# Two-layer streaming encoder on one core: indexer and group A scores in head pairs, output projections in the turned banks

## The reference

```python
# group A: 8 query heads, 2 kv heads; keys picked by a 4-head indexer
dots  = einsum('bqhd,bld->bqhl', iq, ik_all)                 # 4 indexer heads, 64 wide
score = einsum('bqh,bqhl->bql', iw, relu(dots)) * IDX_SCALE  # one score per query and key
score = where(admissible, score, -inf)                       # chunk-causal
_, idx = top_k(score, 256)
s = einsum('bqngd,bqknd->bqngk', qg, k_sel) * 64 ** -0.5     # 2 kv heads x 4 query heads
o_a = einsum('bqngk,bqknd->bqngd', softmax(s), v_sel)
# group B: 4 heads, 1 kv head, a window of 3 chunks of 64, a sink per head
# group M: 4 heads over 256 memory tokens
y = concat([o_a, o_b, o_m]) * silu(gate)
x = x + einsum('btm,md->btd', y, w_out)                      # 1024 -> 1024
```

## Time and profile before

| what | value |
|---|---|
| median of 3 runs | 1681.35 us (1676.07 to 1683.68) |
| profiled execution | 1682.72 us, span 1680.9 us |
| PE busy | 1509.8 us, 90% of the span |
| PE weight loads (beside the products) | 832.3 us, 50% |
| DVE busy | 907.1 us, 54% |
| ACT busy | 659.9 us, 39% |
| POOL busy | 161.2 us, 10% |
| DMA | 114 MB, mean 68 GB/s |
| L697 PE, QUERIES/GATE/KEYS and OUT | 388.4 + 234.0 us |
| L827 PE, scores of A | 183.8 us |
| L794 PE, scores of the indexer | 93.7 us |

### The profile page before, as it was taken

The page is one execution under the profiler, slowest core; times in us unless marked ns, Lnnn a source line. Parts: engine busy times, 40 slices in busy tenths (PEclk is TensorE's granted clock), DMA queues, the critical chain, the costliest instruction groups (busy, mean ns, idle before and its releaser), DMA issues. The chain is left out here.

```text
span 1680.9 us, 19527 instructions
## 1 busy us (share of the span) xinstructions
PE 1509.8 (90%) x6364; PEld 832.3 (50%) x6364; DVE 907.1 (54%) x2361; ACT 659.9 (39%) x1628; POOL 161.2 (10%) x191
## 2 busy tenths in 40 slices
PE   2999999999859999999779999999995799999992
PEld 1544456666524455544434444666664345555451
DVE  0444527887526566656224444488773456666543
ACT  1223426776523333433112242477664233343332
POOL 0100013300000000000001000132000000000003
PEclk9999799999879999999779997999997899999986
DMA  7211310120322111111051004003005121111106
GB/s 270 56 41 33 133 47 1 57 83 40 139 55 53 51 51 51 51 51 25 22 193 40 22 29 153 25 1 113 39 39 170 36 72 51 51 51 51 25 11 235
DMA packets 122623, 114.04 MB, mean 68 GB/s; under 512 B 56432, under 2 KB 95056, under 8 KB 122448
## 3 DMA queue, kind: packets, MB, share of 16 engines
q1 hardware_dynamic: 122528, 112.84, 20.9%
HBM read 87.13 MB, written 30.10 MB: 70 GB/s over the span
## 5 line engine op out<-in xcount | busy, mean ns | idle before, releaser
L697 PE MATMUL score_ps<-w_slot,hT 128*128 128x512 f32 (+2 forms) x1024 | 388.4, 538 | 5.5 <-DMA w_slot<-in_w_in_dram 5.1
L697 PEld LDWEIGHTS score_ps<-w_slot,hT 128*128 128x128 f32 x1024 | 195.8, 194 | 186.3 <-issue 180.2
L1055 ACT ACTIVATE hT<-hT,neg_top 128x128 f32<-128x128 f32 (+8 forms) x144 | 118.0, 820 | 413.6 <-DVE neg_top L1314 413.1
L697 PE MATMUL score_ps<-w_slot,work 128*128 128x512 f32 x512 | 234.0, 611 | 23.4 <-issue 23.4
L1209 DVE TENSOR_SCALAR_CACHE_REDUCE work<-bias,trial 128x384 f32<-128x384 f32 (+3 forms) x256 | 226.0, 883 | 6.8
L922 ACT ACTIVATE work<-bias,neg_trial 128x768 bf16<-128x768 f32 (+2 forms) x192 | 198.4, 1043 | 67.4 <-DVE neg_trial L1205 67.4
L827 PE MATMUL score_ps<-akT,query_mem 64*128 64x512 f32 (+4 forms) x448 | 183.8, 533 | 7.4 <-ACT prob_bm L1069 6.7
L1305 DVE CUSTOM_DVE_ANT_0 hT<-score_ps,bias 128x128 f32<-128x128 f32 (+8 forms) x144 | 116.1, 806 | 116.3 <-PE score_ps L827 115.1
L697 PEld LDWEIGHTS score_ps<-w_slot,work 128*128 128x128 f32 x512 | 97.1, 195 | 147.2 <-issue 146.9
L768 PE MATMUL score_ps<-hT,w_slot 128*128 128x352 f32 x448 | 135.2, 460 | 1.4 <-ACT gate_raw L1044 1.4
L1110 POOL TENSOR_TENSOR work<-work,norm_sb 128x512 f32<-128x512 f32 (+1 forms) x36 | 42.6, 1183 | 915.9 <-DMA norm_sb<-norm_scratch 915.9
(11 more groups left out here) (181 smaller groups left out, 1741.0 us busy)
## 6 DMA issues: line engine op xcount, KB each, us to landing
gate_raw<-x_scratch SPq DMA_DIRECT2D x32, 512.0 KB, 3.7
w_slot<-in_w_in_dram SPq DMA_DIRECT2D x8, 2048.0 KB, 9.5
gate_scratch<-gate_raw SPq DMA_DIRECT2D x16, 528.0 KB, 2.7
w_slot<-in_w_out_dram SPq DMA_DIRECT2D x4, 2048.0 KB, 10.9
work<-gate_scratch SPq DMA_DIRECT2D x16, 512.0 KB, 4.5
norm_sb<-norm_scratch SPq DMA_DIRECT2D x64, 128.0 KB, 3.3
x_scratch<-gate_raw SPq DMA_DIRECT2D x16, 512.0 KB, 3.7
hT<-x_scratch SPq DMA_DIRECT2D x8, 512.0 KB, 8.0
```

The lines of the kernel that those rows point to most:

```text
L697: last = nc.tensor.matmul(out[:, 0:cols], lhs(k), w[:, k, 0:cols], start=(k == 0), stop=(k == KD - 1))
L1055: nc.scalar.activation(p, p, ACT.Exp, bias=neg_b[0:r, j:j + 1], scale=SM_SCALE, accum_out=sums[t % 2][0:r, sum_cols(i, j):sum_cols(i, j) + ...
```

## The change

- **Indexer.** An INDEX step becomes (tile, pair of heads, 512 keys). The two heads of a pair lie in the two 64-row halves of the array and their products stand one behind the other, into columns 0 to 511 and 512 to 1023 of one score buffer. ACT takes two relus per step, DVE adds two. Tiles with up to 512 keys have two steps, those with 640 to 1024 four, the sample six. The wait for the stores of k and v goes from INDEX to TOPK.
- **Group A scores.** Item (A,g) is now query heads 2g and 2g+1 of both kv heads. QK steps come in rounds of two: the products of the two heads alternate between the two halves and the two score buffers, and the steps before PE's need both buffers free. The PV products of A are 64x128 each, twice as many.
- **OUT** goes into the turned banks, c = 0 into one and c = 1 into the other. It has a turn number of its own, so it waits for the copy of the turn two before it, and the turn two behind it waits for ADD. The ADD step goes behind the next round of QK.
- **MIX** of B and M goes behind the PT pair that follows.
- **SP**: half 0 of the output weights is loaded after four of the eight gate stores; tile 1's rows and half 1 of the weights come behind the two round trips of tile 0.

The diff, cut:

```diff
@@ groups_of
+    if item[1] == "A":
+        ...
+            flat = [(g, b, w) for g in range(2) for b, w in whole]
+            cut = [flat[k:k + 2 * at_once] for k in range(0, len(flat), 2 * at_once)]
+        return [[(2 * u + g, b, w) for g, b, w in part for u in range(2)] for part in cut]
@@ attention_steps
-        nxt = score_steps(i + 2) if i + 2 < len(ITEMS) else []
+        nxt = score_rounds(i + 2) if i + 2 < len(ITEMS) else []
...
                 steps.append(("OUT", t - 1, c))
                 if t + 1 in SEARCHED:
                     steps.append(("MASK", SEARCHED.index(t + 1), c))
-                steps.append(("ADD", t - 1, c))
+                added.append(("ADD", t - 1, c))
             while given < len(nxt) and given * groups <= g * len(nxt):
-                steps.append(nxt[given])
+                steps += nxt[given] + added
+                added = []
...
+                        (last_mixes if s[0] == "MIX" and s[2] else steps).append(s)
@@ plan
+def index_steps(t):
+    return [("INDEX", t, hp, c) for hp in range(IDX_HEADS // 2) for c in range(-(-NKEYS[t] // 512))]
@@ numbered
-        if s[0] in ("MEM", "KEYS", "INDEX", "QUERIES", "GATE", "QK", "OUT", "EXTRA"):
+        if s[0] in ("MEM", "KEYS", "INDEX", "QUERIES", "GATE", "QK", "EXTRA"):
...
-        for q in range({"NORM": 2, "CACHE": 1, "MEM_T": 1, "KEYS_T": 2, "QUERIES_T": 2, "PT": 1
+        for q in range({"NORM": 2, "CACHE": 1, "MEM_T": 1, "KEYS_T": 2, "QUERIES_T": 2, "PT": 1, "OUT": 1
@@ sync
-                    for c in range(2):
-                        sp.dma_start(w_slot[c]...).then_inc(w_out_loaded, 16)
+                        if f == KD // 2 - 1:
+                            w_out_load(0)
...
                     tile_load(0)
-                    tile_load(1)
                     for t in range(TILES):
                         norm_turn(t, 1)
                         norm_turn(t, 0)
-                        if t:
+                        if t == 0:
+                            w_out_load(1)
+                            tile_load(1)
+                        else:
@@ tensor, INDEX
+                            for u in range(2):
+                                half = slice(HD * u, HD * (u + 1))
+                                last = nc.tensor.matmul(out[0:r, 512 * u:512 * u + w],
+                                                        iqT[half, hp, t * P:t * P + r],
+                                                        ikT[half, k0:k0 + w], start=True, stop=True)
@@ tensor, QK
+                                for c in range(0, m, 512):
+                                    w = min(512, m - c)
+                                    for u, out in enumerate(pair):
+                                        half = slice(HD * u, HD * (u + 1))
+                                        last = nc.tensor.matmul(out[0:r, c:c + w], aqT[half, head, t * P:t * P + r],
+                                                                akT[half, k0 + c:k0 + c + w], start=True, stop=True)
@@ tensor, OUT
-                            out = score_buffer(step)
-                            pe.wait_ge(w_out_loaded, 32)
+                            g = turn_use(step)
+                            pe.wait_ge(turn_free[g % 2], g // 2)
+                            out = turn_ps[g % 2].rearrange("p k n -> p (k n)")
+                            pe.wait_ge(w_out_loaded[step[2]], 16)
@@ scalar, INDEX
+                            for k in range(2):
+                                at = slice(512 * k, 512 * k + w)
+                                ins = nc.scalar.activation(index_relu[u % 2][0:r, at], ps[0:r, at], ACT.Relu,
+                                                           scale=iw_abs[0:r, t, 2 * hp + k:2 * hp + k + 1])
```

More of the change, by code:

```diff
@@ L89, in score_steps, with score_rounds @@
     return [("QK", i, j) for j in range(4 if ITEMS[i][1] == "A" else 1)]
+def score_rounds(i):
+    steps = score_steps(i)
+    return [steps[k:k + 2] for k in range(0, len(steps), 2)]
 def attention_steps():
-    steps, late, waiting, held = [], [], [], []
+    steps, late, waiting, held, last_mixes = [], [], [], [], []
     last_group = (len(ITEMS) - 1, len(groups_of(ITEMS[-1])) - 1)
@@ L123, in attention_steps @@
         for g in range(groups):
+            added, made = [], []
             if t and it[1:] + (g,) in OUT_AT[t == SMP]:
@@ L152, in attention_steps @@
             waiting += made
+    steps += last_mixes
     while late:
@@ L177, in plan @@
         steps += index[3:4] + [("ROPE", t)]
-    steps += [("INDEX", NT - 1, h) for h in range(IDX_HEADS)] + [("KEYS_T", SMP)]
+    steps += index_steps(NT - 1) + [("KEYS_T", SMP)]
+    last = index_steps(SMP)
     for h, filler in enumerate([("QUERIES", 0), ("MEM", 0), ("MEM", 1)]):
-        steps += [filler, ("INDEX", SMP, h)]
-    steps.append(("INDEX", SMP, IDX_HEADS - 1))
+        steps += [filler] + last[2 * h:2 * h + 2]
+    assert len(last) == 6
     steps += [("TOPK",), ("MEM_T", 0), ("MEM_T", 1)]
@@ new lines, in _ @@
+                            if what == "A":
+                                if j % 2:
+                                    continue
+                                pair = [score_buffer(step), score_buffer(("QK", i, j + 1))]
+                                k0, m, head = 0 if t < SMP else SEQ, min(NKEYS[t], 1024), 2 * g + j // 2
+                                for c in range(0, m, 512):
[4 more added lines that the diff above has]
+                                                                akT[half, k0 + c:k0 + c + w], start=True, stop=True)
+                                        if c + w == m:
+                                            last.then_inc(score_full, 1)
+                                continue
@@ new lines, in _ @@
+                            out = score_buffer(step)
+                            for hh in range(4):
+                                half = HD * (hh % 2)
+                                rows = slice(half, half + HD)
+                                if what == "B":
+                                    q = bqT[rows, hh // 2, t * P:t * P + r]
+                                    k0 = SEQ if t == SMP else P * max(t - 1, 0)
+                                    k = bkT[rows, k0:k0 + (P if t == 0 else 2 * P if t < SMP else P + DEC)]
+                                else:
+                                    q = mqT[rows, hh // 2, t * P:t * P + r]
+                                    k = mkT[rows, int(t == SMP), hh // 2, :]
+                                last = nc.tensor.matmul(out[0:r, 256 * SLOT[hh]:256 * SLOT[hh] + k.shape[1]], q, k,
+                                                        start=True, stop=True)
@@ L1285, in _ @@
+                            if hp == IDX_HEADS // 2 - 1 and 512 * c + w == n and t < SMP:
+                                link(nc.vector.memset(s[0:CHUNK, w - CHUNK:w], NEG))
                         elif kind == "TOPK":
+                            for b in range(2):
+                                dve.wait_ge(kv_stored[b], 16 * kv_dmas(b, TILES))
                             for t in range(TILES):
@@ L1381, in _ @@
                             r, cols = ROWS[t], slice(512 * c, 512 * (c + 1))
-                            ps, free = scores(("OUT", t, c))
+                            bank, free = turned(("OUT", t, c))
+                            ps = bank.rearrange("p k n -> p (k n)")
                             loads = len(range(t % 2, NORMS, 2)) + t // 2 + len(x_parts(t))
```

148 lines of the change are left out of this document (59 added, 89 removed).

## The result

The changed kernel takes **1760.22 us** (median of 4 runs, 1756.41 to 1765.07) against 1679.71 us before (4 runs): ratio 1.0492, 95% interval 1.0463 to 1.0522. The forecast was 1693 with a range to 1730. The direction was right and the size was not: +80 us came where +12 were expected.

The account below looks back on a forecast made before the run. PE's work was taken to bound attention. Per layer 13.4 - 9.1 - 9.0 + 10.5 = +5.8, two layers +11.6 on the profiled 1682.7, 1694, less 1.4 to the median: 1693 us; range 1648 to 1730 (8 in 10).

Parts of the forecast that it names:

- the indexer's term: Indexer: paired products save PE time, mostly at tiles 6 and 7; -9 us per layer, bounds +3 and -17.
- the walk through attention: Attention: hand walk of the new order with old durations, new PE waits against saved work; +13.4 us per layer.
- the clock: Attention: waits of 1.65 us or more bring half-clock drops, nine at 1.15 us each; +10.5 us per layer.
- The pair at the price of one head: A's scores and indexer: two halves run at once, so a pair costs PE 1.98 us at 1024 columns, like one head.
- The rival of a dearer pair: Rounds and indexer steps: a pair costs more than one head, +15 to 20 us, about 1710; chance 0.05.
- The waits of tile 6: Attention, tile 6: new PE waits of together 12.85 us against less work, so 54.8 us instead of 50.2.
- The same walk for the other tiles: Attention: tile 7 +4.6 us, tile 4 +3.5, tiles 1, 2, 3, 5 and the sample within 0.8 of before.
- The start of attention: Before the first OUT: fewer loads ahead shorten the first round trip, OUT at 482.3; -9.1 us per layer.
- the bound called 0: Start of attention: half the weights still ahead and the first trip taking its old 13.5 us; stated as 0, noted "5 less".
- The fourth: Attention: clock falls between OUTs and stays low, tile 6 under 0.85; 1712 to 1730 us, chance 0.16.

Follow-up runs that it names:

- e6: Changed kernel with copies of turned banks and ADD moved between the first and second head of a round on ACT and DVE: 1704.75 us.
- e5: Changed kernel with ADD ahead of the next round of scores, OUT still in the turned banks: 1723.08 us.
- e12: e6 with ACT's copies of turned banks also moved ahead of the exponentials of B, at all tiles: 1679.18 us.
- e2: Kernel before with only the indexer in head pairs of 512 keys: 1677.23 us, ratio 0.9978.
- e1: Kernel before with only the changed order of loads: 1664.91 us, ratio 0.9906.
- e3: Kernel before with OUT in the turned banks and ADD behind the next head's scores, heads still single: 1769.55 us.
- e8: Kernel before with the changed order of loads and the paired indexer, nothing else: 1666.03 us, ratio 0.9916.
- e4: Changed kernel with OUT back in the score buffers and ADD ahead of the next round; pairs, paired indexer and load order stay: 1698.93 us.
- e7: e4 with copies of turned banks and ADD between the first and second head of a round on ACT and DVE: 1672.29 us.
- e11: e8 (single heads) with ACT's copies of turned banks ahead of the exponentials of B and M where they follow directly: 1652.19 us.

## Why the prediction was wrong

The step that failed first is the indexer's term: PE time was taken as saved wherever PE had been busy. The other two terms that failed, the walk through attention and the clock, had the right mechanism and were too small. All errors lean to the same side. In us per layer:

| term | forecast | layer 0 | layer 1 |
|---|---|---|---|
| to the last gate store (indexer) | -9.0 | 0.0 | +2.0 |
| from there to the first OUT | -9.1 | -7.6 | -7.6 |
| attention without the clock's cost (the walk) | +13.4 | +24.7 | +24.5 |
| the clock's cost in attention | +10.5 | +17.4 | +22.4 |
| behind it | 0 | +1.2 | +1.1 |
| sum | +5.8 | +35.7 | +42.4 |

**The pair at the price of one head.** Right: 1.99 us for a pair of 1024 keys. The rival of a dearer pair is out.

**The waits of tile 6.** Right in sum and, but for one, in cause. The walk had 0.35, 2.2, 2.7, 3.05, 1.65, 0.2 and 2.7, in sum 12.85; PE is idle for 12.84, and the large waits are 0.40, 2.16, 2.99, 2.96, 1.47 and 2.71. The 1.65 was to be a round that waits for M's scores. The trace has 1.47 before a turn, for ACT's copy behind two exponentials; that the sizes agree is luck. In e6 that turn no longer waits, and the next round waits 1.50 us for M's exponentials. The other causes are shown by the runs that move them. In e5 the 2.96 for ADD becomes 1.35 and 0.47 for copies. In e6 the 2.16 becomes 0.96, and the 2.71, which was for ACT's copy, becomes 1.46 for MIX. In e12 the 2.99 is gone.

**The same walk for the other tiles.** Here the sum fell short. Without the clock's cost, attention of layer 0 went from 318.5 to 343.2 us: +24.7 instead of +13.4. Of the 11.3 us missing, 6 are in tiles 1 to 3, where I had forecast nothing (+0.6, -0.4, -0.25) and each became some 2 us longer (+2.2, +1.8, +2.0 without the clock's cost), and 2.1 in tile 7 (+6.7 against +4.6). Tile 2 stands idle for 6.5 us of its 37.5: 1.90 for ADD, 1.54 for M's exponentials, 1.22 and 1.03 before OUT for copies, 0.79 before M's scores. So the small tiles have the kinds of wait that the large ones have. That they have less PE work to hide them is my reading; no run takes it apart.

**The clock.** The mechanism was right and the term of +10.5 per layer too small. I took nine drops of 3.4 us. Attention of layer 0 has twelve stretches below full clock, where it had three before, so nine more is what came. Ten of them last 3.4 to 4.3 us and cost 1.5 to 1.7 us each; the others are that of the first OUT and one of 21 us at the sample, of which 15 us lie in attention and cost 6.6 (4.3 before). I had counted each drop at 1.15 because the next wait would give back a third. At the full 1.7 nine drops are 15 us, and that is most of what was missing in layer 0. In tile 6, with two drops, the waits add up to the 12.84 us that the walk had without any, so there nothing was given back. Layer 1 has two more stretches of some 7 us (3.0 and 2.6) near its end.

**The indexer.** The step that failed outright: -9 per layer was forecast, and to the end of the gates layer 0 came out 0.5 us shorter; alone (e2) the pairs gave 2.6 us in both layers. I let PE's saved time count wherever PE had been busy, though the turns and projections wait for copies on DVE that stand behind the indexer's sums. 15 us less busy time became 17 us more idle time.

**The start of attention.** Right in cause, near in size: the second half of the first trip was issued at 464.78 and that of the second at 475.88, forecast 465 and 475.3; the first OUT came at 483.77, forecast 482.3. From the last gate store to the first OUT the gain is 7.6 us in both layers against the 9.1 forecast, and 8.8 and 8.5 in e1, where nothing else is changed (15 us in all). In the prediction the bound called 0 is worked out as 5 less; that slip changed nothing.

**The rivals.** The fourth (clock low for long) describes the sample's 21 us and e3's 18 us, but tile 6 had a granted clock of 0.94, not under 0.85, so it isn't what made the 80 us. Those are, for a layer, 24.6 of waits less saved work, some 20 of clock, less 6 to 8 up to the first OUT. The upper end of 1730 failed because terms that lean to the same side were each taken at their middle: indexer 9 to 11, walk 11, clock 7 to 12, start 1.5 and the way behind attention 1 make 30 to 37 per layer.

**What the two parts of the attention change are worth.** With the new loads and the paired indexer everywhere: single heads, OUT in score buffers 1666 (e8); pairs, OUT in score buffers 1699 (e4); pairs, OUT in turned banks 1760 (after). Against before without those two: single heads, OUT in turned banks 1770 (e3). In attention of layer 0 e3 and the changed kernel differ by -34 us of work and +35 of idle time, at about the same cost of the clock. So with OUT in the turned banks what the pairs save goes into waits, while in the score buffers they cost 33. That figure holds the moved MIX of B and M as well, which no run tests alone; and with single heads the place of OUT and the place of ADD were not tried apart. With the copies in the right place (e7 and e12) the pairs still don't beat single heads (e11). Of the 42 us of idle time that remain in attention of e7, 13.5 are rounds that wait for M's exponentials, 10.2 are rounds that wait for ADD, and 8.9 are OUT half 0 behind A's MIX. Kernels that take M's scores out of the way, or put A's MIX between the two heads, weren't tried, so it stays open whether pairs could beat single heads.

## What to carry to other kernels

When the bound engine gets work taken away, walk its neighbours' in-order queues through every period, not only the largest: time is saved only where the next wait is not already there. Before moving a tile between buffers, ask which queue empties the buffer and what stands ahead of that copy; moving the copy ahead of exponentials that PE did not need so soon was worth 14 us in the kernel with single heads and 22 in the one with pairs. And take a change apart: two of its parts (the loads, and a little of the indexer) were gains hidden under a loss of 94 us (1666 in e8 against 1760).

## What the runs showed of the hardware

A short wait can cost twice. In the changed kernel the stretch behind a wait of 3 us has half clock with PE busy without a gap:

```profile
737.50:741.80 4.30, 4.30 (x30) 3.52 (x32) 1.03 (x2) 1.15 (x4) 0.00 (x0) 0.60 0.47 164
```

Not every wait does. Behind the first OUT of layer 0 the changed kernel has 17 waits of PE of 1.65 us or more. At ten of them such a stretch begins, during the wait or within 2 us behind it, at seven none does; the shortest of the ten is 1.72 us and the longest of the seven 2.70, so the length of the wait alone doesn't tell. Tiles 2 and 3, with 6.5 and 6.8 us of waits, stay at full clock (1.00 in both).

Usually a stretch is over after 3.4 to 4.3 us and costs 1.5 to 1.7. But in e3 one lasted 17.9 us of full PE work behind a wait of 1.64 us and cost 8.5, and one 10.3 us behind a wait of 1.60 us and cost 5.1. The longer one stood where two waits (2.96 before OUT, 1.64 behind the next scores) ended 13 us apart. Which of the outcomes a wait brings, these runs don't settle.
